# An MLP computed in two stages, each product made of seven quarter products, instead of one fused stage

## What is computed

```python
def _finish(x, oa, ob, w_o, g_mlp, w_up, w_down):
    bn, t = x.shape[:2]
    o = jnp.concatenate([oa.reshape(bn, t, D_A), ob.reshape(bn, t, D_B)], axis=-1).astype(x.dtype)
    x = x + o @ w_o
    u = jax.nn.relu(_rmsnorm(x, g_mlp) @ w_up)
    return x + (u * u) @ w_down
```

## Time and profile before

| | us |
|---|---|
| median of 3 runs | 3653.38 (3651.86 to 3654.7) |
| the profiled execution, its own time | 3653.38 |
| its span, first to last instruction | 3647.8 |
| PE busy | 3465.1, 95% of the span |
| DVE busy | 1491.2, 41% |
| ACT busy | 1123.8, 31% |
| POOL (GpSimd) busy | 1099.6, 30% |
| mean granted TensorE clock | 0.980 |
| HBM traffic | 156 GB/s over the span |

### The profile page before, as it was taken

How to read it: one execution, slowest core, us unless ns; L and a number is a source line. 1 busy time by engine, 2 the same in 40 slices (tenths; PEclk the granted TensorE clock), 3 DMA queues, 4 the chain that set the end, 5 groups by cost and what they waited for, 6 DMA issues and landing times. The chain is left out here.

```text
span 3647.8 us, 50724 instructions
## 1 busy us (share of the span) xinstructions
PE 3465.1 (95%) x18240; PEld 2687.8 (74%) x18240; DVE 1491.2 (41%) x2874; ACT 1123.8 (31%) x1664; POOL 1099.6 (30%) x1029
## 2 busy tenths in 40 slices
PE   7999999799997999899989999999999999999999
PEld 7987788555554666654437788888877888888888
DVE  2223333466545766243323434333333334343333
ACT  3322223245553667522214311111113211111111
POOL 1223456577775666501331100000101100000000
PEclk9999999899998999899989999999999999999999
DMA  5546667876655677489953211111113111111111
GB/s 194 200 164 205 215 209 217 204 200 195 189 163 149 171 201 208 162 323 331 321 190 135 76 51 46 46 46 46 46 70 136 47 47 46 46 46 46 34 35 64
DMA packets 301228, 503.45 MB, mean 138 GB/s; under 512 B 48594, under 2 KB 190420, under 8 KB 295636
## 3 DMA queue, kind: packets, MB, share of 16 engines
q1 hardware_dynamic: 264052, 366.09, 33.3%
q10 hardware_dynamic: 23032, 80.04, 6.5%
q0 software_dynamic: 13952, 54.80, 4.1%
HBM read 403.98 MB, written 164.50 MB: 156 GB/s over the span
## 5 line engine op out<-in xcount | busy, mean ns | idle before, releaser
L2988 DVE TENSOR_TENSOR fin_x<-mlp_y,fin_x 128x512 f32<-128x512 f32 x544 | 350.2, 686 | 756.4 <-PE mlp_y L3033 756.4
L2948 POOL TENSOR_TENSOR mlp_u<-fox_in_squares 128x1024 f32<-128x1024 f32 (+2 forms) x80 | 132.4, 1655 | 1319.0 <-ACT fox_in_squares L2889 1319.0
L3033 PE MATMUL mlp_y<-fin_w_hi,mlp_u_lo 128*128 128x512 f32 x1088 | 426.2, 392 | 0.0
L681 PE MATMUL proj_z<-proj_w_lo,proj_x_hi 128*128 128x512 f32 (+1 forms) x816 | 304.0, 373 | 0.0
L680 PE MATMUL proj_z<-proj_w_hi,proj_x_hi 128*128 128x512 f32 (+1 forms) x748 | 281.2, 376 | 11.1 <-DVE proj_w_lo L519 10.7
L682 PE MATMUL proj_z<-proj_w_hi,proj_x_lo 128*128 128x512 f32 (+1 forms) x748 | 276.0, 369 | 0.0
L3033 PEld LDWEIGHTS mlp_y<-fin_w_hi,mlp_u_lo 128*128 128x128 f32 x1088 | 201.3, 185 | 49.5
L3031 PE MATMUL mlp_y<-fin_w_hi,fox_in_w 128*128 128x512 f32 (+1 forms) x576 | 227.9, 396 | 4.6 <-DVE fin_x L2988 4.6
L2882 ACT ACTIVATE fin_w_hi<-fin_w_raw 128x1024 fp32r<-128x1024 f32 x124 | 128.2, 1057 | 320.9 <-PE mlp_y L3033 166.4
L3032 PE MATMUL mlp_y<-fin_w_lo,fox_in_w 128*128 128x512 f32 (+1 forms) x576 | 227.1, 394 | 0.0
L3008 PE MATMUL mlp_u_more<-fin_h_hi,fin_w_hi 128*128 128x512 f32 (+2 forms) x640 | 224.8, 351 | 2.1 <-PEq L55 2.1
(11 more groups left out here) (319 smaller groups left out, 7619.5 us busy)
## 6 DMA issues: line engine op xcount, KB each, us to landing
samp_v_in<-in_cache_v POOLq DMA_DIRECT2D x128, 256.0 KB, 4.9
fin_w_raw<-in_w_up SPq DMA_DIRECT2D x64, 512.0 KB, 3.9
fin_w_raw<-in_w_down SPq DMA_DIRECT2D x64, 512.0 KB, 4.0
out_new_win_k<-in_win_k ACTq DMA_DIRECT2D x8, 4080.0 KB
out_new_win_v<-in_win_v ACTq DMA_DIRECT2D x8, 4080.0 KB
samp_k_in<-in_cache_k SPq DMA_DIRECT2D x80, 256.0 KB, 5.0
proj_x_hi<-scratch_xt SPq DMA_DIRECT2D x34, 512.0 KB, 4.9
proj_x_lo<-scratch_xt SPq DMA_DIRECT2D x34, 512.0 KB, 5.8
```

The source lines that it names most:

```text
L681: pe.matmul(out, x_hi[:, slot, xs], w_lo[p % 2][k][:, ws], start=False, stop=False)
L2988: dve.tensor_tensor(part, y_ps[(tiles * par + t) % 2][0:rows, q * D_G:(q + 1) * D_G], part, ALU.add).then_inc(y_added, 1)
L3033: mm = pe.matmul(out, lo, w_hi[:, par, 2 + f, b_], start=False, stop=(f == FB - 1))
```

## The change

`finish` now runs three stages, each with its own SBUF, and each starts when the stores of the one before have landed.

**`join_heads`** runs once over all 17 tiles, so w_o is split once. Its x1 tiles go to DRAM (`scratch_x`). For each pair of tiles GpSimd makes four sums of quarters (make_t), and seven operands go to DRAM (`scratch_hc`, the samples' h to `scratch_hs`).

**Seven products for eight.** Two matrices cut into 2x2 quarters normally need eight products of quarters; here seven products of sums of quarters are made (Winograd's form of Strassen), numbered 1 to 7 and made in the order 1, 5, 6, 2, 7, 3, 4. Each still takes three matmuls per 128 rows. They accumulate in three chains of PSUM banks (CHAIN): 1, 6, 7, 4 in one bank, 5 and 3 in a second, 2 in a third; there are two sets, used by turns. A bank in a chain is read between two of its products, since its running sum is an intermediate result. The prompt's 2048 rows are two token groups.

**`mlp_up`**: 32 steps (2 groups, 16 blocks of 256 features). A step makes seven products of 12 matmuls, 512 columns each (L3163 to L3166), 84 in all. ScalarE copies the chain-0 bank after products 1, 6 and 7 (t1, t2, t3, L3007) and takes relu directly after product 4 (L3003); VectorE adds bank and copy after 2, 7 and 3 (L3115); ScalarE takes relu of these (L2988 of the new kernel), GpSimd squares. GpSimd also makes four sums of w_up quarters (make_s) and four of squared u (make_su) per step. Every weight part is split as before. Seven stores of 256 KB per step go to `scratch_uc`. TensorE's product 3 waits (free_bank) for VectorE's read of the bank after product 7, and that read waits for ScalarE's copy t3 of product 7.

**`mlp_down`**: 64 units of one pair of tiles (256 rows), in 16 quarters of w_down, called q here, of 4 units each (u = 0 to 3). A unit is seven products of 6 matmuls, 512 columns each, 42 in all. ScalarE copies the chain-0 bank after 1, 6, 7 and 4 (L3368), GpSimd adds the copy into the accumulator in SBUF, VectorE adds products 5, 2 and 3 from PSUM. Per unit ScalarE and VectorE split u (hi_u, lo_u, parts of 768 and 1024 elements), per q they split seven w parts of 1024 elements, four of them sums that GpSimd makes first (make_t, 128x1024). A w load is 2 MB (L3260), a u load 896 KB (L3267), three u slots.

**The samples** are left out of the seven products: in `mlp_up` 16 plain float32 matmuls (64 rows, 128 columns) and a transpose per step of the second group, in `mlp_down` 8 (512 columns) per q of the second group.

The diff, cut to its core (`join_heads` keeps its shape but for what is said above; `mlp` and `token_chunks` are removed):

```diff
-    for g, (first, tiles) in enumerate(GROUPS_T):
...
-            join_heads(nc, c, dram, g, first, tiles, h_hi, h_lo, x1, o_in, o_loaded[g], w_in, u_first, sent)
-            mlp(nc, c, dram, g, first, tiles, h_hi, h_lo, x1, w_in, u_first, o_in, o_loaded[1], spare, sent)
...
+ORDER = (1, 5, 6, 2, 7, 3, 4)
+POS = {k: i for i, k in enumerate(ORDER)}
+CHAIN = {1: 0, 6: 0, 7: 0, 4: 0, 5: 1, 3: 1, 2: 2}
+NP = len(ORDER)
+QUARTER = 4 * P
+N_GROUPS_T = 2
+PAIRS_T = TILES // 2 // N_GROUPS_T
+BLOCKS = D_FF // FBLK
+KBLOCKS = BLOCKS // 2
...
+            def make_t(u):
+                (b11, b12), (b21, b22) = of_pair(u)
+                pool.wait_ge(hg_done, 2 * (2 * u + 2))
+                pool.wait_ge(tc_sent, 64 * u)
+                pool.tensor_tensor(tc[:, 0, :, :], b12, b11, ALU.subtract).then_inc(t_made, 1)
+                pool.wait_ge(t_made, 4 * u + 1)
+                pool.tensor_tensor(tc[:, 1, :, :], b22, tc[:, 0, :, :], ALU.subtract).then_inc(t_made, 1)
+                pool.tensor_tensor(tc[:, 2, :, :], b22, b12, ALU.subtract).then_inc(t_made, 1)
+                pool.wait_ge(t_made, 4 * u + 3)
+                pool.tensor_tensor(tc[:, 3, :, :], b21, tc[:, 1, :, :], ALU.subtract).then_inc(t_made, 1)
...
+def mlp_up(nc, c, dram, wr, wr_loaded, h_lo, h_loaded, o_in, spare):
...
+            for n in range(STEPS_N):
+                if n + 2 < STEPS_N:
+                    sp.wait_ge(w_split, entry(n, 4) + 1)
+                    sp.wait_ge(s_made, 4 * (n + 1))
+                    if sampled(n):
+                        sp.wait_ge(s_done, n - BLOCKS + 1)
+                    load_w_up(sp, dram, wr, wr_loaded, n + 2)
...
+            for k in ORDER:
+                hi_h(0, k)
+                hi_w(POS[k])
+            for e in range(1, len(seq) + 2):
+                if e <= len(seq):
+                    n, k = seq[e - 1]
+                    if k in ACT_READS:
+                        act.wait_ge(product, e)
+                        bank = c_ps[0][n % 2]
+                        if k == 4:
+                            if n > 0:
+                                act.wait_ge(u_sent[C21], 16 * n)
+                                act.wait_ge(su_made, 4 * n)
+                            act.activation(u[:, C21, :], bank[:, :], ACT.Relu).then_inc(read_act, 1)
+                        else:
+                            if n > 0:
+                                act.wait_ge(read_dve, 3 * (n - 1) + {1: 1, 6: 3, 7: 2}[k])
+                            act.activation({1: t1, 6: t2, 7: t3[:, :]}[k], bank[:, :], ACT.Copy).then_inc(read_act, 1)
+                if e >= 2:
+                    n, k = seq[e - 2]
+                    if k in DVE_READS:
+                        relu(n, {2: C11, 7: C22, 3: C12}[k])
...
+                if e + AHEAD - 1 < len(seq):
+                    hi_w(e + AHEAD - 1)
...
+            def make_su(n):
+                pool.wait_ge(sq_done, 4 * (n + 1))
+                if n > 0:
+                    pool.wait_ge(su_sent, 64 * n)
+                pool.tensor_tensor(su[:, 0, :], u[:, C12, :], u[:, C22, :], ALU.add).then_inc(su_made, 1)
+                pool.wait_ge(su_made, 4 * n + 1)
+                pool.tensor_tensor(su[:, 1, :], su[:, 0, :], u[:, C11, :], ALU.subtract).then_inc(su_made, 1)
+                pool.tensor_tensor(su[:, 2, :], u[:, C11, :], u[:, C12, :], ALU.subtract).then_inc(su_made, 1)
+                pool.wait_ge(su_made, 4 * n + 3)
+                pool.tensor_tensor(su[:, 3, :], u[:, C21, :], su[:, 1, :], ALU.subtract).then_inc(su_made, 1)
...
+                elif k in (6, 7, 4):
+                    pe.wait_ge(read_act, 4 * n + ACT_READS[k] - 1)
...
+                elif k == 3:
+                    pe.wait_ge(read_dve, 3 * n + 2)
...
+def mlp_down(nc, c, dram, wr, o_in, spare):
...
+    RING = NP + 4
+    U_SLOTS = 3
+    FILLS = [[], [(2, 0), (6, 1)], [(2, 2), (6, 3)], [(2, 4), (6, 5)]]
+    LATE = (2, 6)
...
+            for m in range(UNITS):
+                q, u = divmod(m, UNITS_Q)
+                g = q // KBLOCKS
+                if u == 0 and q + 1 < Q_N:
+                    sp.wait_ge(w_split, NP * (q + 1))
+                    if sampled(q):
+                        sp.wait_ge(s_done, q - KBLOCKS + 1)
+                    load_w(q + 1)
...
+                if m >= 1 and m + 2 < UNITS:
+                    sp.wait_ge(product, NP * m)
+                    load_u(m + 2)
...
+            for m in range(UNITS):
+                fills = filled_in(m)
+                for pos, k in enumerate(ORDER):
+                    if k in ACT_READS:
+                        s = 4 * m + ACT_READS[k] - 1
+                        act.wait_ge(product, NP * m + pos + 1)
+                        if s >= 2:
+                            act.wait_ge(pool_added, s - 1)
+                        act.activation(out[s % 2], c_ps[0][m % 2][:, :], ACT.Copy).then_inc(read_act, 1)
+                    if m + 1 < UNITS and pos in (0, 4):
+                        hi_u(m + 1, pos // 4)
+                    if pos in fills:
+                        hi_w(fills[pos])
...
+            for m in range(UNITS):
+                q, u = divmod(m, UNITS_Q)
+                for k, (i, j, after) in ((1, (0, 0, 2)), (6, (0, 1, 3)), (7, (1, 1, None)), (4, (1, 0, None))):
+                    pool.wait_ge(read_act, 4 * m + ACT_READS[k])
...
+                    pool.tensor_tensor(to, out[(4 * m + ACT_READS[k] - 1) % 2], to, ALU.add).then_inc(pool_added, 1)
+                    if (u, k) in ((1, 1), (1, 6), (2, 6), (2, 4)):
+                        make_t(q + 1, [(1, 1), (1, 6), (2, 6), (2, 4)].index((u, k)))
...
+                    if pos == 0 and late is not None:
+                        lo_w(late)
+                    if pos in (1, 5) and m + 1 < UNITS:
+                        lo_u(m + 1, pos // 5)
+                    if pos == 3 and 2 in fills:
+                        lo_w(fills[2])
...
+                elif k in (6, 7, 4):
+                    pe.wait_ge(read_act, 4 * m + ACT_READS[k] - 1)
...
+                elif k == 3:
+                    pe.wait_ge(dve_added, 3 * m + 1)
...
+def finish(nc, c, dram, ph, o_in, o_loaded, spare):
+    wr_loaded, h_loaded = ph.sems("wr_loaded"), ph.sems("h_loaded", NP)
+    with Phase(nc, "fin") as ahead:
+        wr = ahead.sb("wr", [P, 2, KC, FBLK])
+        with Phase(nc, "fin_h") as of_h:
+            h_lo = [of_h.sb(f"h_lo{k}", [P, 4, QUARTER], F32R) for k in range(NP)]
+            join_heads(nc, c, dram, o_in, o_loaded, wr, wr_loaded, h_lo, h_loaded)
+            mlp_up(nc, c, dram, wr, wr_loaded, h_lo, h_loaded, o_in, spare)
+        mlp_down(nc, c, dram, wr, o_in, spare)
```

897 lines of the change are left out of this document (590 added, 307 removed).

## The result

| | before | changed kernel |
|---|---|---|
| median | 3654.0 (4 runs) | 3704.3 (4 runs, 3701.7 to 3716.8) |
| ratio | | 1.0132, 95% interval 1.0108 to 1.0156 |
| profiled execution, its own time | 3653.4 | 3703.2 |
| span | 3647.8 | 3701.6 |

The change makes the kernel slower by 1.3%, 50 us. I had forecast slower, but by 23 us only; the 3704 lies inside the range of 3605 to 3735, but the loss is about twice the one forecast. One thing is needed to read all that follows: the part of the program ahead of join_heads is the same in all kernels, yet the first transpose of join_heads came between 1910.3 and 1932.7 us in the fourteen profiles (1913.15 before, 1917.0 in the changed kernel). So small differences are read stage by stage, not from totals.

The account below looks back on a forecast made before the run. PE was taken to bound the kernel (95% busy), so only fewer matmuls could give much. The stage terms from 1913 us summed to 1758.0 against 1734.8, +23.2, so 3677 us, 0.6% slower; range 3605 to 3735.

Parts of the forecast that it names:

- Join, once: join_heads run once over all tiles: 225.4 us, bounds 222 and 232 if GpSimd's sums hold VectorE back.
- first step: First step of mlp_up: 39 us, seven h quarters split before all its products are made; bounds 32 and 46.
- change of group: mlp_up, at the second token group: 12 us, seven h quarters loaded and split again beside one PE step; bounds 0 to 25.
- 14 q's: mlp_down's steady q's: 46.3 us each, 648 in all, PE's own part 38.1; ends 38.1 and 50.
- 31 further steps: mlp_up after its first step: 20.8 us each, 644.8 in all, with a 1.6 wait ahead of product 3.
- term (a): mlp_down, each q: u load queued behind the late w load delays product 7 of unit 1; 5.0 us idle.
- (b): mlp_down, each q: after the idle time the clock runs at half rate for 3.4 us; +1.6 us.
- Term (c): mlp_down, each q: GpSimd and VectorE share an SBUF port; 1.6 us for what doesn't fit beside the idle time.
- B: Rival, faster: in mlp_down neither load nor port holds PE, a q is 38.1; 115 less, 3562; chance 0.11.
- C: Rival, slower: mlp_up's 32 idle times of 1.7 turn the clock down; 1.7 more per step, +54, 3731; chance 0.07.
- A: Rival: only part of the load, clock and port costs bears, a q is 43.4; 41 less, 3636; chance 0.20.
- D: Rival: shared port as exclusive lock in mlp_down, 47.3 per q, 48.9 in 14 with the clock; +36, 3713; chance 0.12.

Follow-up runs that it names:

- both load edits: Against the changed kernel, in mlp_down: seventh w part split at the end of the q before, and u load issued ahead of the w load; 3649.7, ratio 0.9991.
- narrow additions: Against the changed kernel: GpSimd's additions in mlp_down handle 64 of 512 columns, rest of that accumulation left out, load order kept; 3696.6, one run.

## Why the prediction was right in direction and short in size

The signs, the places and the releasers in the steady steps and q's held; the sizes did not add up. I forecast +23.2 against the span; it came to 1788.6 - 1734.8 = +53.8, of which 4.0 stand ahead of the change. The terms, in us, added up where the prediction had them apart:

| term | forecast | measured |
|---|---|---|
| 1913.0 to join_heads (the code is unchanged) | 0 | 4.0 |
| Join, once, to its last product | 225.4 | 224.7 |
| join to mlp_up's first operation | 14 | 14.7 |
| first step, from there | 39 | 39.9 |
| further steps, samples, change of group | 688.8 | 703.6 |
| to mlp_down, and its first q | 76 | 78.3 |
| 14 q's with samples and change of group | 669.2 | 677.2 |
| last q and tail | 45.6 | 46.2 |
| sum | 1758.0 | 1788.6 |

- **Join, change of stage and first step** held to 0.9 us together. The boundaries are those of the prediction: join ends with its last product, and mlp_up begins with ScalarE's first copy of h. (The parts named for the first step, 29.4 + 3 + 2.5 + 2.7, make 37.6 and not 39.)

```profile
2141.43 0.39 PE L2836 MATMUL join_pr<-join_w_hi,join_o_lo 128*128 128x512 f32 x1
...
2156.36 1.91 ACT L2977 ACTIVATE up_h_hi<-fin_h_h_lo 128x2048 fp32r<-128x2048 f32 x1 [10.03 <-PEq L55]
```

- **Change of group** (mis-sized by 5.5): "7 x 2.28 on VectorE beside one step" came to steps of 31.2 and 32.8. Both carry samples, whose matmuls are made one step ahead, and such a step usually takes 23.2: 17.5 in place of 12. Of these 13.4 are longer waits, and 4.1 are matmuls 0.43 apart behind them, the half clock, which this term left out:

```profile
2513.67 0.77 PE L3163 MATMUL up_c<-up_h_hi,up_w_hi 128*128 128x512 f32 x1 [8.00 <-DVE up_u L3115]
...
2545.28 0.77 PE L3163 MATMUL up_c<-up_h_hi,up_w_hi 128*128 128x512 f32 x1 [8.34 <-DVE up_u L3115]
```

  The subtractions of 2048 elements took 2.72 on the mean, not 2.28, some of them beside GpSimd: 3.1 us more on VectorE. With products 3 and 4 exchanged the change of group still cost 16.1 (29.9 and 31.1, where 22.4 is usual).
- **31 further steps** came 20.96 apart for 20.8, 5 us in all, and the samples cost 2.27 per step for 2.0, 4 us.
- **14 q's**, the largest single miss: term (a), the load, and (b), the clock, held together to 0.3 us. Term (c), the port, is the step that failed: "I take 1.6 for what doesn't" fit beside the idle time. It was 48.03 - 45.02 = 3.0 in q without samples and nothing in those with samples; and for the samples I took 2.25 where they showed as 0.6, since they covered the port. So in the q's with samples two errors cancelled by luck: 46.3 + 2.25 = 48.55 forecast, 48.63 measured. The six q's without samples took 10.4 more than forecast and those with samples 0.6; the change of group lies within these and did not ask for the 3 allowed: +8.0 in the sum.

**The rivals.** B fell as forecast. C fell: with 1.95 from matmul to matmul once in each step the clock stayed 1.00. It was near: in the run with both load edits a wait of 2.42 from start to start in q 4 was followed by matmuls 0.43 apart (from 3131.37), while in its q's with samples waits of 2.3 left the clock at 1.00 from 3267.7 to 3574.9. A fell: both the load and the port were there. D gave 3713 and is the nearest number to the 3704, but not for its reason: it counted 47.3 per q for the port alone, and with the load nearly out of the way a q took 44.06, all those operations in it. The Trainium skill, "SBUF — State Buffer", section "SBUF: two separate sides", calls the shared pair an exclusive lock for the whole instruction, whoever starts first, if VectorE has two inputs in SBUF; the rows with 2.44, 2.28 and 1.30 agree in both directions to 0.15 us. What is not right is to add up the lengths of all records and call it a bound. That the port is given back somewhat before a record's end would account for it (3.2 us or more over 35 operations). In the three rows the one held up ends 0.13 to 0.15 us sooner than the other's end and its own length alone (1.22, 1.28, 0.33) would give, which fits, but no run here tests it.

## What to carry to other kernels

Fewer matmuls help only as far as the work that forms their operands fits beside them: here 12.5% fewer products brought GpSimd and VectorE close to TensorE's time on one port, and two causes of 6.9 and at most 6.0 us hid in part behind one another, so that neither showed its full worth alone. Take two such causes away together before giving a change up. Where a load waits for the last use of a buffer and another stands behind it in the queue, issue first what is free first; and when work is moved into an idle time, move what hangs on its result too, since a square of 0.4 us behind a sum that waits cost 4 us per step.

## What was not expected of the hardware

- The load wait and the port's lag overlapped only in part (6.9 and at most 6.0 make 9.9). The plain float32 matmuls of the samples, 3.7 us per q, covered all of the port's lag in the changed kernel (48.63 against 48.80 with narrow additions), and half of it with the load edits in: a q took 44.06 without and 44.74 with them, 2.9 over 41.8.
- With the sums on VectorE the port's count is 37.5 us (12 additions of 1.28, 19 operations of VectorE) in a q of 39.8, nearly as tight as before, and yet TensorE waits only 1.3 us in a q without samples; GpSimd's additions took 1531 ns there, not 1279.
- Moving a sum from GpSimd to VectorE halves its hold on the port, 1284 ns against 2863 in the changed kernel for the first of the two kinds.
